# Recurrent mixer: the next batch's features and the running product's first value on GpSimd, rates' sigmoids first, the decay scale inside the exponentials

## What is computed

```python
def wkv7_scan(r, decay, k, v, kk, a, reverse):
    def step(s, inp):
        r_t, w_t, k_t, v_t, kk_t, a_t = inp
        s = (s * w_t[:, :, None, :]
             - jnp.einsum('bhij,bhj->bhi', s, kk_t)[..., None] * (kk_t * a_t)[:, :, None, :]
             + v_t[..., None] * k_t[:, :, None, :])
        return s, jnp.einsum('bhij,bhj->bhi', s, r_t)
...
w_log = -softplus(-(w0 + tanh(wd) @ w_up)) - 0.5
decay = exp(-exp(w_log))
a = sigmoid(a0 + ad @ a_up)
k_dir = k * (1.0 + (a - 1.0) * k_a)
# forward and backward scans, each with its own decay and a
```

## Time and profile before

| | us |
|---|---|
| median of 3 executions | 3335.96 |
| lowest and highest | 3335.18, 3340.79 |
| span of the profiled execution | 3341.8 |
| the same, PE busy | 3229.7 (97%) |
| the same, DVE busy | 2441.0 (73%) |
| the same, ACT busy | 1296.1 (39%) |
| the same, POOL busy | 86.1 (3%) |

### The profile page before, as it was taken

How to read it: one execution, slowest core, us unless ns; L and a number is a source line. 1 busy time by engine, 2 the same in 40 slices (tenths; PEclk the granted TensorE clock), 3 DMA queues, 4 the chain that set the end, 5 groups by cost and what they waited for, 6 DMA issues and landing times.

```text
span 3341.8 us, 62748 instructions
## 1 busy us (share of the span) xinstructions
PE 3229.7 (97%) x25596; PEld 3036.0 (91%) x25596; DVE 2441.0 (73%) x4488; ACT 1296.1 (39%) x2435; POOL 86.1 (3%) x116
## 2 busy tenths in 40 slices
PE   8999999999988999999999999999999889999998
PEld 7999999888776999999989999998877669999997
DVE  6877777654879577677887877776458876776766
ACT  5333334222445443333543343342134634333333
POOL 0001100000000000000001000000000000000000
PEclk9999999999999999999999999999999989999999
DMA  3222223221042222222222312232300521122221
GB/s 111 70 84 77 88 70 120 74 100 66 4 153 108 76 64 70 66 75 65 75 70 81 94 57 84 82 117 70 120 24 22 199 80 50 61 71 76 67 76 70
DMA packets 89262, 266.27 MB, mean 80 GB/s; under 512 B 10152, under 2 KB 18472, under 8 KB 87696
## 3 DMA queue, kind: packets, MB, share of 16 engines
q1 hardware_dynamic: 84656, 248.35, 22.6%
q0 software_dynamic: 4320, 13.91, 1.4%
HBM read 232.33 MB, written 29.88 MB: 78 GB/s over the span
## 4 chain that ended last, share of the span: by engine, by line
PE 87%; DVE 8%; issue 2%; ACT 1%; DMA 1%; SPq 0%; POOL 0%; DVEq 0%; ACTq 0%
PE ps L1031 51%; PE ps L1111 36%; DMA wring<-wa 1%; DVE wl L2417 1%; PE ps L1607 0%; DVE sc L3070 0%; DMA x<-xT 0%; DVE uv L3022 0%; DVE gl L2611 0%; DVE x L2320 0%; DVE M2X L2793 0%; ACT sqb L1718 0%; DVE sc L3081 0%; DVE olocal L2919 0%; DVE Mrk L2780 0%
## 5 line engine op out<-in xcount | busy, mean ns | idle before, releaser
L1111 PE MATMUL ps<-gh,wh 128*128 128x384 f32 x2488 | 839.1, 337 | 24.2 <-DVE gl L2616 13.7
L1111 PE MATMUL ps<-gh,wl 128*128 128x384 f32 x2488 | 834.5, 335 | 0.0
L1111 PE MATMUL ps<-gl,wh 128*128 128x384 f32 x2488 | 834.5, 335 | 0.0
L1111 PEld LDWEIGHTS ps<-gh,wh 128*128 128x128 f32 x2488 | 468.9, 188 | 33.1 <-issue 10.5
L1031 PE MATMUL ps<-act_high,wh 128*128 128x384 f32 x1408 | 478.4, 340 | 2.0 <-DVE act_low L2483 2.0
L1031 PE MATMUL ps<-act_high,wl 128*128 128x384 f32 x1408 | 471.9, 335 | 0.0
L1031 PE MATMUL ps<-act_low,wh 128*128 128x384 f32 x1408 | 471.8, 335 | 0.0
L1111 PEld LDWEIGHTS ps<-gl,wh 128*128 128x128 f32 x2488 | 469.2, 189 | 0.5
L1111 PEld LDWEIGHTS ps<-gh,wl 128*128 128x128 f32 x2488 | 469.1, 189 | 0.0
L2320 DVE SCALAR_TENSOR_TENSOR x<-ps,x 128x384 f32<-128x384 f32 x416 | 227.1, 554 | 225.1 <-PE ps L1031 224.6
L1739 ACT CAST wh<-wring 128x512 fp32r<-128x512 f32 (+2 forms) x260 | 183.2, 706 | 466.3 <-PE ps L1031 389.7
(11 more groups left out here) (306 smaller groups left out, 4973.0 us busy)
## 6 DMA issues: line engine op xcount, KB each, us to landing
wring<-wa SPq DMA_DIRECT2D x244, 512.0 KB, 3.5
wring<-wa SPq DMA_DIRECT2D x128, 256.0 KB, 2.6
wring<-wa SPq DMA_DIRECT2D x64, 192.0 KB, 2.3
bias<-bias SPq DMA_DIRECT2D x24, 512.0 KB, 7.6
conv_q_k<-stage SPq DMA_DIRECT2D x28, 384.0 KB, 2.5
kern_rows<-kst POOLq DMA_DIRECT2D x24, 256.0 KB, 3.4
outT<-x SPq DMA_DIRECT2D x2, 3072.0 KB, 9.7
kern<-kern_rows SPq DMA_DIRECT2D x12, 512.0 KB, 7.2
```

The lines of the kernel that those rows point to most:

```text
L1111: m = pe.matmul(out, lhs[a], rhs[b], start=start and n == 0, stop=stop and n == 2, skip_group_check=onto)
```

## The change

GpSimd takes over, for all four batches, the steps `rate`, `key`, `ksum`, `keys`, `alpha`, `feat_ab`, `rho` and `feat` (new function `features`), and the first value of X (events `one`), which PE waits for ahead of stage 4. DVE keeps `scan` and `cum`, now one step earlier in the table, and the small copy of each chunk's last decay (`ends`). The step `decay` is gone; the exponentials get DECAY_SCALE as their scale. PE and ACT make the two rate pieces first and the two decay pieces after them. PE's batch q now waits for GpSimd's event `feat`.

```diff
-        PREPARE_AT = {(4, 1): "decay", (5, 0): "scan", (5, 1): "cum", (5, 2): "rate", (6, 0): "key", (6, 1): "ksum", (6, 2): "keys",
-                      (7, 0): "alpha", (7, 2): "feat_ab", (8, 0): "rho", (8, 2): "feat"}
+        PREPARE_AT = {(4, 1): "scan", (5, 0): "cum", (7, 2): "ends"}
...
+            def features(l, q):
+
+                d, i = divmod(q, 2)
+                F, rates, M = feat[q % 2], kap[:, :, :].rearrange("p c t -> p (c t)"), ALU.mult
+                in_chunks = lambda t: t.rearrange("p (c t) -> p c t", t=CH)
+                pool.wait_ge(*ra_.at(l, "sig", q, 3 if q == 0 else 1))
+                pool.tensor_scalar(rates, tmp[:, 1, :], prm("rwkv_k_a", i), dpar[:, 16 + i:17 + i], M, ALU.add)\
+                    .then_inc(*rg.inc(l, "rate", q))
...
+                pool.wait_ge(*ra_.at(l, "expE", q))
+                pool.tensor_tensor(F[:, :, ALPHA, :], in_chunks(kk[:, i, :]), in_chunks(tmp[:, 0, :]), M)\
+                    .then_inc(*rg.inc(l, "alpha", q))
+                pool.wait_ge(*rg.at(l, "keys", q))
+                pool.wait_ge(*ra_.at(l, "expN", q))
+                pool.tensor_tensor(F[:, :, BETA, :], F[:, :, BETA, :], in_chunks(tmp[:, 2, :]), M)\
+                    .then_inc(*rg.inc(l, "feat_ab", q))
+                pool.tensor_tensor(F[:, :, RHO, :], in_chunks(pa[:, i, :]), in_chunks(tmp[:, 3, :]), M)\
+                    .then_inc(*rg.inc(l, "rho", q))
+                pool.tensor_tensor(kap[:, :, :], kap[:, :, :], in_chunks(tmp[:, 2, :]), M).then_inc(*rg.inc(l, "feat", q))
...
+                features(l, 0)
+                for q in range(4):
+                    for g in range(GROUPS):
+                        h = slice(4 * g, 4 * g + 4)
+                        pool.wait_ge(*rv.at(l, "b", q, 0, g))
+                        pool.tensor_tensor(M2X[:, h, 1, :], sq_a[:, h, :], eye_b(4), ALU.add)\
+                            .then_inc(*rg.inc(l, "one", q, g))
+                    if q < 3:
+                        pool.wait_ge(*rp.at(l, "b", q, 1, GROUPS - 1))
+                        features(l, q + 1)
...
+                if s == 4:
+                    pe.wait_ge(*rg.at(l, "one", q, g))
...
-                t0, tn = SEGS[k // 2]
-                mm(bank(7, tn), *lora_operands(q, k % 2, t0, tn)).then_inc(*rp.inc(l, "lora", q, k))
+                t0, tn = SEGS[k % 2]
+                mm(bank(7, tn), *lora_operands(q, 1 - k // 2, t0, tn)).then_inc(*rp.inc(l, "lora", q, k))
...
-                A(tmp[:, 0, :], tmp[:, 0, :], ACT.Exp).then_inc(*ra_.inc(l, "expE", q))
+                A(tmp[:, 0, :], tmp[:, 0, :], ACT.Exp, scale=DECAY_SCALE).then_inc(*ra_.inc(l, "expE", q))
...
-                    m = TT(X, sq_a[:, h, :], eye_b(4), AD)
```

More of the change, by code:

```diff
@@ L446, in k_rv @@
                 out += [("ksq", i), ("kmax", i), ("vt", i), ("kk", i)]
-            out += [("cum", 0), ("keys", 0), ("feat_ab", 0), ("feat", 0)]
+            out += [("cum", 0), ("ends", 0)]
             for q in range(4):
@@ L460, in k_rv @@
                             out += [("bonus", s - 4)]
-                        if q < 3 and PREPARE_AT.get((s, g)) in ("cum", "keys", "feat_ab", "feat"):
+                        if q < 3 and PREPARE_AT.get((s, g)) in ("cum", "ends"):
                             out += [(PREPARE_AT[s, g], q + 1)]
@@ L473, in build, with k_rg @@
         FILTER_JOBS = [FILTER_AT[u] for u in sorted(FILTER_AT)]
+        def k_rg():
+            made = lambda q: [(n, q) for n in ("rate", "key", "ksum", "keys", "alpha", "feat_ab", "rho", "feat")]
+            return made(0) + [e for q in range(4) for e in [("one", q, g) for g in range(GROUPS)] + (made(q + 1) if q < 3 else [])]
         def k_fp():
@@ L1460, in rwkv @@
                 for q in range(4):
-                    pe.wait_ge(*rv.at(l, "feat", q))
+                    pe.wait_ge(*rg.at(l, "feat", q))
                     for s in range(BATCH):
@@ L1995, in sigmoid_part @@
                 if k == 0:
[L1996 to L1998 removed]
+                    sa.wait_ge(*rg.at(l, "feat", q - 1))
+                (t0, tn), a = SEGS[k % 2], 1 - k // 2
+                A(tmp[:, a, t0:t0 + tn], bank(7, tn), ACT.Sigmoid, bias=prm(("rwkv_w0", "rwkv_a0")[a], q))\
+                    .then_inc(*ra_.inc(l, "sig", q, k))
             def exps(l, q):
@@ L2810, in prepare @@
             def prepare(l, q, part):
-                d, i = divmod(q, 2)
-                F, kf = feat[q % 2], flat(kap[:, :, :])
-                if part == "decay":
+                if part == "scan":
                     ve.wait_ge(*ra_.at(l, "sig", q, 3))
-                    step(TS(tmp[:, 0, :], tmp[:, 0, :], DECAY_SCALE, None, M))
-                elif part == "scan":
                     if q < 2:
@@ L2823, in prepare @@
                     TT(tmp[:, 0, :], tmp[:, 2, :], tmp[:, 0, :], SU).then_inc(*rv.inc(l, "cum", q))
[L2824 to L2835, removed]
[L2836 to L2850 removed]
+                else:
+                    d, i = divmod(q, 2)
+                    ve.wait_ge(*ra_.at(l, "expL", q))
+                    ve.tensor_copy(pc[d][:, i, :], by_chunk(tmp[:, 3, :])[:, :, CH - 1 if d == 0 else 0]).then_inc(*rv.inc(l, "ends", q))
             def key_square(l, i):
@@ L3151, in _ @@
                     scale_qk(l, i)
-                    for part in {1: ("decay", "scan", "cum"), 2: ("rate", "key", "ksum", "keys"), 3: ("alpha", "feat_ab"),
-                                 4: ("rho", "feat")}.get(i, ()):
+                    for part in {1: ("scan", "cum"), 4: ("ends",)}.get(i, ()):
                         prepare(l, 0, part)
```

32 lines of the change are left out of this document (15 added, 17 removed).

## The result

| | before | changed |
|---|---|---|
| median of 4 executions, taken in turn | 3338.38 | 3352.07 |
| lowest and highest | 3335.18, 3340.85 | 3347.74, 3355.53 |
| span of the profiled execution | 3341.8 | 3348.7 |
| the same, DVE busy | 2441.0 | 2410.5 |
| the same, POOL busy | 86.1 | 212.7 |

The changed kernel takes 1.0036 times as long (1.0022 to 1.005), which is 12.0 us; the medians differ by 13.7 us, where +7.0 was forecast. 3352 lies outside the range, which ended at 3350. Of the 9 us between it and the forecast of 3343, 2.4 are the kernel before itself, whose median is 3338.38 here and was 3335.96 where the forecast began. Most of the loss is in the two mixers: from the first product of batch 0 to the first product behind batch 3 the profiled execution takes 3.8 us more in layer 0 and 7.6 us more in layer 1.

The account below looks back on a forecast made before the run. PE and DVE were each nearly full and waiting for the other. Per layer 2 x 1.6 + 0.8 - 0.5 = +3.5 us, two layers +7.0, on the median 3336.0: 3343 us; range 3328 to 3350 for 8 in 10.

Parts of the forecast that it names:

- Exponentials 0.2 us earlier: Batch 1, stages 4 to 6: ACT's table load moves earlier and the exponentials end at 866.6 instead of 866.8.
- A multiplication of 1.8 us: GpSimd's 768-column multiplication, in no row, taken as 1.8 us between 1.4 and 2.2; features ready 6 us early.
- Three turns, the last addition 2.05 us later: Before stage 8, DVE's three additions to NR alternate with GpSimd's multiplications; the last ends at 872.9 against 870.85.
- The free DVE worth 0.9 us in batches 0 and 1: Stages 7 to 10 if GpSimd were silent: stage 10 could start about 0.9 us before 874.38.
- Stages 9 and 10 follow it in PE's order. Batches 0 and 1: +1.6 us each.: PE's third group of stage 8 starts at 872.9 instead of 871.29, and that delay carries on through stage 10.
- the walk: Instant-by-instant timeline of batch 1, giving DVE's and GpSimd's turns before stage 8: PE 1.6 us later.
- Batch 2: +0.8: Batch 2: +0.5 from the same meeting at stage 8 and +0.3 from chain steps' additions meeting `key` or `ksum`.
- Batch 3: -0.5: Batch 3 makes no features, so it keeps the gain of stage 2: 0.5 us shorter.
- The sum: Both layers: 2 x 1.6 + 0.8 - 0.5 = +3.5 us each, two layers +7.0, giving 3343 us.
- two turns: Rival, chance 0.25: DVE asks before GpSimd's second multiplication and meets only two; +0.5 a layer, 3337 us.
- a silent meeting: Rival, chance 0.2: DVE's additions go in between GpSimd's without waiting; 2.8 us gained a layer, 3330 us.
- a late GpSimd: Rival, chance 0.1: GpSimd's last four multiplications end after the next batch's start at 880; 3355 us or more.

Follow-up runs that it names:

- second trace: The changed kernel run again unedited and profiled once more, beside the kernel before: 3353.16 us, ratio 1.004.
- PE kept at work: Changed kernel with unread 128x512 products on PE in all three waits for the additions to NR, batches 0 and 1: 3354.54 us, ratio 1.0037.
- GpSimd nearly silent: Changed kernel with GpSimd's last four multiplications in batches 0 to 2 cut to one chunk of twelve: 3339.37 us, ratio 0.9996.

## Why the prediction was wrong in size and right in direction

- **Exponentials 0.2 us earlier:** 22.40 to 22.21. Right.
- **A multiplication of 1.8 us:** 1.80 to 1.99 in batch 1 (group means up to 2.2 over the whole span). Right; in time for the next batch by 9 us.
- **Three turns, the last addition 2.05 us later:** 26.46 to 28.49, +2.03. Right, with its cause: without the meeting (three experiments) the loss is gone, and a late addition without GpSimd brings it back.
- **The free DVE worth 0.9 us in batches 0 and 1:** 0.8 to 1.4 at stage 10 where it could show.
- **"Stages 9 and 10 follow it in PE's order. Batches 0 and 1: +1.6 us each."** This step failed. Stage 10 was late by 3.4, 2.95, 3.4 and 1.7 us, 11.4 in sum where 6.4 stood, and by 12.7 in the second trace. Two things are in it. Batch 0's last addition came at 26.07 before, not at batch 1's 26.46, so it lost 2.4 instead of 2.0; the walk was made on one batch and carried to the other. And the clock fell to 0.50 in three of the four, +1.3 each (in all four in the second trace); the fourth, where it did not, is the +1.7 that goes with the walk's 1.6. With PE kept at work the four are late by 7.6 in sum. Of the 11.4 us, 6.4 are left at the next stage 1, which is the forecast's sum, but by luck: 5.0 us came back at the borders, 2.6 of them at the one where the kernel before was slow. In the second trace 11.1 are left.
- **Batch 2: +0.8.** In the first trace this step failed more: +1.95 and +3.34 us, 5.3 in two layers against 1.6. In the second trace, without a late batch 2, it is +1.1 and +0.7, as forecast. The part "the chain steps' additions, as at 892.95, can now meet `key` or `ksum`" named the mechanism and took its price, "+0.3, from bounds of -0.5 and +1.5", from the wrong side of the scan: where the meeting comes, the chain's PE step waits for the addition (1.38 us), long before the scan, the clock falls for 3.4 us, and the exponentials ended 3.2 us later (0.9 in layer 0, where there was no such wait). Bound and value were both too small.
- **Batch 3: -0.5.** The third addition is 0.33 us earlier in both layers. The batch as a whole is 0.47 us shorter in layer 0 and 0.11 longer in layer 1, since PE's "issue" waits inside stage 10 changed too (1.07 to 0.80, 0.80 to 1.08).
- **The sum.** By the second table, +6.4 for batches 0 and 1, +5.3 for batch 2 and -0.4 for batch 3 are the 11.4 us of the two mixers, where 6.4 + 1.6 - 1.0 = 7.0 stood; the second trace has +11.1, +1.8 and -1.2, in sum 11.7. The medians differ by 13.7 and 12.1 in two series. The spans of the profiled pair differ by 6.9 only, 4.5 less than their mixers, but that of the second trace by 12.5: some us come and go outside the mixers.
- **The chances.** By its own cases they are 0.10 faster and 0.52 same, not 0.12 and 0.5.

Of the rivals, neither two turns nor a silent meeting nor a late GpSimd came; the range failed because its upper end came from the multiplication's length alone (to 3349), while the clock behind a wait of 2.4 us was not in the walk, and the batch 2 term was held to be small.

Still open: what PE waits for in its "issue" gaps at the border, which the profile does not show. How much of the late batch 2 is `rate` and how much `key` was not taken apart further, and what the fallen clock costs the whole kernel was not settled.

## What to carry to other kernels

Before work goes to GpSimd, look at which DVE instructions with both inputs in SBUF it will run beside, and who waits for those: the short ones on the critical path pay for a whole GpSimd instruction each, here four times their own length. Let the critical one read from PSUM, or start GpSimd's work behind it; and judge every batch that differs (here the one with chain steps) by a walk of its own, up to stage 1 of the next one, since waits at a border change too. Before a loss is shared out among its parts, take a second trace of the same kernel: here the total was the same and the parts were not.

## What the runs showed of the hardware that was not expected

- PE idle for 2.4 us was followed by a granted clock of 0.50 over some 7 us (872 to 879), in three of the four batches 0 and 1 of one execution. In the fourth PE waited 2.41, 1.05 and 1.05 us in the same places and the clock stayed at 1.00. In the second execution it fell in all four, for 3.4 or 6.8 us. With gaps of 0.76 and 1.73 us between groups it stayed at 1.00 in three batches of four and fell for 3.4 us in the other.
- Shorter waits were followed by 0.50 too, in some batches: 1.39 us at the border of the kernel before (3.4 us at 0.50, from 882.2), 1.19 us in the kernel with GpSimd nearly silent (6.8 us). Behind the 1.10 us at 841.36 it stayed at 1.00.
- One 768-column multiplication of GpSimd held up a 128-column addition of DVE for 1.66 instead of 0.29 us, and a 768-column operation with one tensor input in SBUF (`rate`, 0.98 us) did so too, for 0.97.
- PE's unexplained wait at a batch's start was 0.50 us in one trace of the changed kernel and 1.39 in the other, at the same border.
